# Two edits to a two-block network kernel: when VectorE builds a pair's selection, and where the gates' product runs

## The reference

```python
scores = sigmoid(xt @ router_w)                     # the 8 chosen experts of each token come from these
hb = silu(xb @ w_gate[e]) * (xb @ w_up[e])          # xb: the rows routed to expert e
y = (hb @ w_down[e]) * ws[:, None]
```

```python
x = x + 0.5 * swiglu(rms_norm_2(x, norm_ffn1[l]), ffn1_in[l], ffn1_out[l])
h = rms_norm_2(x, norm_mix[l])
p_rwkv, p_attn, p_gate = split(h @ w_in[l])         # p_gate: 256 x 2048
o_a = rwkv7_mixer(p_rwkv, ...)                      # a linear recurrence over tokens, forward and backward
o_b = diff_attention(p_attn, ...)                   # 4 heads, two softmax maps each
y = einsum('bsgc,gcd->bsgd', stack([o_a, o_b]), w_branch[l])
merged = sum(sigmoid(p_gate) * y, over the two branches)
x = x + merged @ w_out[l]
x = x + 0.5 * swiglu(rms_norm_2(x, norm_ffn2[l]), ffn2_in[l], ffn2_out[l])
```

## Time and profile before

| what | us |
|---|---|
| three runs | 4134.38, 4137.35, 4137.35 |
| their median | 4137.35 |
| the profiled execution's own time | 4137.76 |
| its span in the trace | 4136.1 |
| first block (both layers) | 0 to about 2046 |
| second block (both layers) | about 2046 to the end |
| PE busy | 3485.1 |

### The profile page before, as it was taken

The page is one execution under the profiler, slowest core; times in us unless marked ns, Lnnn a source line. Parts: engine busy times, 40 slices in busy tenths (PEclk is TensorE's granted clock), DMA queues, the critical chain, the costliest instruction groups (busy, mean ns, idle before and its releaser), DMA issues.

```text
span 4136.1 us, 46292 instructions
## 1 busy us (share of the span) xinstructions
PE 3485.1 (84%) x18496; PEld 2414.5 (58%) x18496; DVE 1569.9 (38%) x2703; ACT 842.4 (20%) x1240; POOL 599.4 (14%) x556
## 2 busy tenths in 40 slices
PE   6888999994788899999299958798988994879899
PEld 3754333331566333333098648686978963877688
DVE  4433222224634222222354265531545426554154
ACT  1211111110130111111132221111324223111132
POOL 4402233331440233233100000000000000000000
PEclk8889999997878999999699968779998996877999
DMA  7647999985754899889554300004536430000352
GB/s 264 236 158 279 364 347 354 356 338 197 283 181 168 343 351 353 341 350 358 181 195 153 130 8 1 1 21 147 199 102 225 159 117 21 1 1 13 130 204 102
DMA packets 305420, 799.38 MB, mean 193 GB/s; under 512 B 57030, under 2 KB 155868, under 8 KB 251308
## 3 DMA queue, kind: packets, MB, share of 16 engines
q1 hardware_dynamic: 245804, 727.16, 46.8%
q0 software_dynamic: 58848, 67.05, 4.9%
q10 hardware_dynamic: 544, 2.10, 0.1%
HBM read 989.01 MB, written 53.48 MB: 252 GB/s over the span
## 4 chain that ended last, share of the span: by engine, by line
PE 41%; DVE 6%; ACT 1%; issue 1%; DMA 1%; SPq 0%; DVEq 0%
PE s_bank L1899 12%; PE s_bank L1937 6%; PE s_bank L1887 5%; PE s_bank L2083 2%; PE s_bank L1964 2%; PE s_bank L2098 2%; PE s_bank L2093 1%; PE s_bank L2200 1%; PE s_bank L2210 1%; PE s_bank L2168 1%; PE s_bank L2160 1%; PE s_bank L2071 1%; DMA s_ringA<-in_ffn_in 1%; PE s_bank L2153 1%; PE s_bank L2145 1%
## 5 line engine op out<-in xcount | busy, mean ns | idle before, releaser
L711 PE MATMUL f_bank<-f_ringA,f_arena 128*64 128x512 f32 x3072 | 688.7, 601 | 16.3 <-DMA f_ringA<-in_w_up,f_chosen 10.1
L711 PEld LDWEIGHTS f_bank<-f_ringA,f_arena 128*64 128x64 f32 x3072 | 222.3, 138 | 401.4 <-issue 400.1
L1899 PE MATMUL s_bank<-s_hT_high_parts,s_highA_parts 128*128 128x256 f32 x1408 | 402.7, 286 | 17.7 <-DVE s_hT_parts L2428 17.7
L1899 PE MATMUL s_bank<-s_hT_parts,s_highA_parts 128*128 128x256 f32 x1408 | 402.2, 286 | 0.0
L1899 PE MATMUL s_bank<-s_hT_high_parts,s_ringA_parts 128*128 128x256 f32 x1408 | 402.0, 285 | 0.0
L732 PE MATMUL f_bank<-f_ringB,f_arena 128*64 128x512 f32 x1536 | 346.5, 592 | 1.0 <-DVE f_arena L1473 1.0
L1012 ACT ACTIVATE f_arena<-f_bank 128x512 f32<-128x512 f32 (+1 forms) x362 | 202.1, 587 | 575.1 <-PE f_bank L692 174.2
L1465 DVE TENSOR_TENSOR f_arena<-f_arena,f_bank 128x256 f32<-128x256 f32 x96 | 58.6, 610 | 636.3 <-ACT f_arena L1090 636.3
L1899 PEld LDWEIGHTS s_bank<-s_hT_high_parts,s_highA_parts 128*128 128x128 f32 x1408 | 274.2, 195 | 20.4 <-issue 19.0
L1899 PEld LDWEIGHTS s_bank<-s_hT_parts,s_highA_parts 128*128 128x128 f32 x1408 | 274.3, 195 | 1.4
L1899 PEld LDWEIGHTS s_bank<-s_hT_high_parts,s_ringA_parts 128*128 128x128 f32 x1408 | 274.1, 195 | 0.0
(11 more groups left out here) (393 smaller groups left out, 5361.2 us busy)
## 6 DMA issues: line engine op xcount, KB each, us to landing
f_ringA<-in_w_gate SPq DMA_DIRECT2D x128, 1024.0 KB, 8.7
f_ringA<-in_w_up SPq DMA_DIRECT2D x128, 1024.0 KB, 11.1
f_ringB<-in_w_down SPq DMA_DIRECT2D x128, 1024.0 KB, 12.3
s_ringA<-in_ffn_in SPq DMA_DIRECT2D x88, 1024.0 KB, 7.7
f_ringA<-in_w_ada SPq DMA_DIRECT2D x48, 1024.0 KB, 8.4
s_arena<-in_ffn_out SPq DMA_DIRECT2D x44, 1024.0 KB, 6.0
s_ringA<-in_w_in SPq DMA_DIRECT2D x40, 1024.0 KB, 6.1
f_ringA<-in_w_in SPq DMA_DIRECT2D x28, 1024.0 KB, 10.2
```

What stands on the lines that cost most here:

```text
L711: last = mm(ps[j * CAP:(j + 1) * CAP, :].rearrange("p (h c) -> p h c", h=2), picked[:, b % 2, k, j * CAP:(j + 1) * CAP], gu[j][:, :, k, :] ...
L1899: last = mm(ps[:, t * S:(t + 1) * S], parts_of(wx[:, k, cs_]), parts_of(hx[:, k, :]), start=(k == 0 and x == 0), stop=(k == DT - 1 and x = ...
```

## The change

In the first block `select(b + AHEAD)` moves on VectorE from behind the copies of iteration b to the head of the iteration, ahead of the wait for the SiLU. `take_rows` stays.

In the second block:

- The gates' product is cut into 16 pieces (`half_gates`), each 8 matmul calls. Pieces 0 to 7 stand behind the scores of attention's steps 0 to 7; pieces 8 to 15 behind the chunk steps of the scans, four a direction. The loop over 8 groups after the scans is gone.
- ACT takes groups 0 to 3 as plain copies during attention, one sigmoid over them (2048 columns) behind the set-up of direction 0, and groups 4 to 7 through a sigmoid in the scans. No take waits for `oa_ready` any more.
- `gates` moves into slot 0 of `ringA`. The gate and branch weights use slots 1 and 2 in turn (`slot_of`); `w_out` gets two places of its own in SBUF that the scans have used, so its loads wait for the last Y bank.
- Three instead of one of ffn2's first weights are loaded before `x_ready`.

```diff
@@ first block, VectorE
                 for b in range(PAIRS + 1):
+                    if b + AHEAD < PAIRS:
+                        select(b + AHEAD)
                     if b < PAIRS:
                         dve.wait_ge(silu_ready, b + 1)
...
                     if b + AHEAD < PAIRS:
-                        select(b + AHEAD)
                         take_rows(b + AHEAD)
@@ second block, buffers, banks and slots
-        gates = view(base + 1024, 4096, "p (t s) -> p t s", s=S)
+        gates = ringA[:, 0, :].rearrange("p (t s) -> p t s", s=S)
+        w_out = [view(base + 8192 + 4096 * n, 4096) for n in range(2)]
...
+        for g in range(4):
+            banks.take(("gates", g), 2 + g % 2)
...
+            for g in range(4 + 2 * d, 6 + 2 * d):
+                banks.take(("gates", g), 4 + g % 2)
...
-        for g in range(8):
-            banks.take(("gates", g), g % 4)
...
+        slot_of = [n % slots_A for n in range(a_gate)] + [1, 2] * 3 + [(1, 2, 0)[s % 3] for s in range(STEPS)]
@@ SP
                 def slot_free(n):
-                    if n >= slots_A:
-                        banks.read(sp, last_use[n - slots_A])
+                    before = [i for i in range(n) if slot_of[i] == slot_of[n]]
+                    if before:
+                        banks.read(sp, last_use[before[-1]])
+                    if n == a_ffn2 + 2:
+                        sp.wait_ge(merged, DT)
...
+                banks.read(sp, ("Y", 1, 1))
                 for c in range(2):
-                    load(a_out + c, rows8(slotA(a_out + c)),
-                         a["w_out_2"][l, :, c * 512:(c + 1) * 512].rearrange("(k p) c -> p k c", p=P))
-                load_up(2, 0)
+                    dst = rows8(w_out[c])
+                    src = a["w_out_2"][l, :, c * 512:(c + 1) * 512].rearrange("(k p) c -> p k c", p=P)
+                    for h in range(2):
+                        sp.dma_start(dst[:, h * 4:(h + 1) * 4], src[:, h * 4:(h + 1) * 4]
+                                     ).then_inc(each[f"w_out{c}"], 16)
+                for s in range(3):
+                    load_up(2, s)
                 sp.wait_ge(x_ready, 2)
                 for s in range(STEPS):
-                    if s:
+                    if s >= 3:
                         load_up(2, s)
                     load_down(2, s)
@@ PE
+            def half_gates(i):
+
+                g, t = i // 2, i % 2
+                c = a_gate + g // 2
+                if i % 4 == 0:
+                    landed(c)
+                ps = banks.claim(pe, ("gates", g)) if t == 0 else banks.t[banks.uses[("gates", g)][0]]
+                w, o = rows8(slotA(c)), (2 * (g % 2) + t) * P
+                for k in range(DT):
+                    last = mm(ps[:, t * S:(t + 1) * S], w[:, k, o:o + P], hT[:, k, :],
+                              start=(k == 0), stop=(k == DT - 1))
+                if t:
+                    banks.fill(last, ("gates", g))
...
                         banks.fill(last, ("score", s))
+                        half_gates(s)
                     if s % 2 and s > 1:
...
+                        half_gates(8 + 4 * d + n)
                     pe.wait_ge(sa_ready, 4 * d + 4)
...
-                for g in range(8):
-                    c = a_gate + g // 2
-                    if g % 2 == 0:
-                        landed(c)
-                    o = (g % 2) * 2 * P
-                    ps = banks.claim(pe, ("gates", g))
-                    banks.fill(hidden(ps, rows8(slotA(c))[:, :, o:o + 2 * P]), ("gates", g))
                 pe.wait_ge(oa_ready, 1)
@@ ACT
                         last.then_inc(exp_done, 1)
+                        if s % 2:
+                            take_gates(s // 2, ACT.Copy)
...
+                    if d == 0:
+                        for g in range(4):
+                            banks.evacuated(act, ("gates", g))
+                        f(gates[:, 0:8, :], gates[:, 0:8, :], ACT.Sigmoid).then_inc(gates_ready, 1)
+                    for g in range(4 + 2 * d, 6 + 2 * d):
+                        take_gates(g, ACT.Sigmoid)
 
                 roots(16)
-                for g in range(8):
-                    if g == 0:
-                        act.wait_ge(oa_ready, 1)
-                    take(("gates", g), gates[:, 2 * g:2 * g + 2, :], pair_of, ACT.Sigmoid)
@@ VectorE
-                for g in range(8):
+                dve.wait_ge(gates_ready, 1)
+                for g in range(4, 8):
                     banks.evacuated(dve, ("gates", g))
```

More of the change, by code:

```diff
@@ L1621, in second_block @@
                  "highA_ready", "lowA_ready", "highB_ready", "lowB_ready", "hT_split", "hid_split",
-                 "oa_ready", "merged", "dve_steps", "rows_landed", "arrived"]
+                 "oa_ready", "gates_ready", "w_out0", "w_out1", "merged", "dve_steps", "rows_landed", "arrived"]
         names += [f"bank_filled{i}" for i in range(8)] + [f"bank_freed{i}" for i in range(8)]
@@ L1641, in second_block @@
         merged, dve_steps, arrived = each["merged"], each["dve_steps"], each["arrived"]
+        gates_ready = each["gates_ready"]
         rows_landed = each["rows_landed"]
@@ L1737, in second_block @@
         a_wa = a_gate + 4
-        a_wb, a_out, a_ffn2 = a_wa + 1, a_wa + 2, a_wa + 4
+        a_wb, a_ffn2 = a_wa + 1, a_wa + 2
         last_use = {s: ("u", 0, s) for s in range(STEPS)}
@@ L1743, in second_block, with a_filled @@
         last_use |= {a_wa: ("branch", DT - 1), a_wb: ("branch", DT - 1)}
-        last_use |= {a_out + n: ("out", n, 1) for n in range(2)}
         last_use |= {a_ffn2 + s: ("u", 2, s) for s in range(STEPS)}
         ffn_first = {0: 0, 2: a_ffn2}
+        slot_of = [n % slots_A for n in range(a_gate)] + [1, 2] * 3 + [(1, 2, 0)[s % 3] for s in range(STEPS)]
         def slotA(n):
-            return ringA[:, n % slots_A, :]
+            return ringA[:, slot_of[n], :]
+        def a_filled(eng, n):
+            eng.wait_ge(a_landed[slot_of[n]], 32 * slot_of[:n + 1].count(slot_of[n]))
         def rows8(ap):
@@ L1778, in load @@
                         sp.dma_start(dst[:, h * half:(h + 1) * half], src[:, h * half:(h + 1) * half]
-                                     ).then_inc(a_landed[n % slots_A], 16)
+                                     ).then_inc(a_landed[slot_of[n]], 16)
                 def load_up(f, s):
@@ L1869, in landed @@
             def landed(n):
-                pe.wait_ge(a_landed[n % slots_A], 32 * (n // slots_A + 1))
+                a_filled(pe, n)
             def to_features(key, src, n_banks):
@@ L2204, in _ @@
                 for n in range(2):
-                    landed(a_out + n)
-                    w = rows8(slotA(a_out + n))
+                    pe.wait_ge(each[f"w_out{n}"], 32)
+                    w = rows8(w_out[n])
                     for m in range(MT):
@@ L2229, in take, with take_gates @@
                 banks.free(f(dst, view_(banks.read(act, key)), func, **kw), key)
+            def take_gates(g, func):
+                take(("gates", g), gates[:, 2 * g:2 * g + 2, :], pair_of, func)
             def split_up(k, s):
                 n = ffn_first[k] + s
-                act.wait_ge(a_landed[n % slots_A], 32 * (n // slots_A + 1))
+                a_filled(act, n)
                 if s >= 2:
```

## The result

The changed kernel takes **3979.06 us** (3978.22 to 3982.74, 4 runs) against 4136.94 us (4134.38 to 4137.35, 4 runs) before: ratio 0.962, 95% interval 0.9607 to 0.9633, 158 us less. The forecast was 4037 us, range 3995 to 4090. The direction was right; the gain was half as large again as forecast, and it lies outside the range.

What follows compares the result with a forecast made beforehand. TensorE, busy 84%, was limited differently by stage: selection waits in the first loop, VectorE in attention, the gates' product after the scans. From 4137.76 us, -68 - 81.8 + 19 + 30 = -100.8 gave 4037 us, range 3995 to 4090.

Steps and rivals of the forecast that it cites:

- First part: First block's loop: moving the selection removes the lookup's 0.90 us wait, 77.7 us traced, less 10 for late weights: -68.
- The bound of -78: First block's loop: the most the moved selection could save, all of the lookup's traced wait.
- the 64 of the second part: Second block: us saved with the gates' product change at its best, used for the range's lower end.
- Rival 2: First block's loop: transfers bound it, so the moved selection saves 34 for 68 us; 4071 us, chance 12%.
- What goes after the scans: Y's last bank to branches: 17.3 us for 60.8 without the gates' product, -43.5; cold branches +2.6 a layer.
- Attention: Eight pieces a layer: first head pair's combination after 20.2 us, +9.4; later heads 11.3 us, as now; +9.5 a layer.
- Scans: Four pieces a direction: step 0 +5.9, steps 1 and 2 +1.5 each, step 3 +2.5, Y sums -4; +7.4 a direction.
- if the clock holds: Scan steps 1 and 2: 8.8 us, no change, at a held clock; 12.9, +4, if it falls; +1.5 each taken.
- a rise within each piece: Scans: full-width work raises the clock to 1.00 once per piece, as at 2407.6 in attention; what follows takes about half.
- Rival 1: Clock sags in the scans: each direction +19, attention +15 us a layer; 4094 us, chance 20%.
- Rival 3: Scans and attention: every piece runs whole at 1.2 GHz, making the kernel slower; 4181 us, chance 5%.
- Rival 4: No effect: another wait replaces the selection's, scans and attention eat the 41 us a layer; about 4138 us, chance 2%.

Runs made afterwards that it cites:

- e1_select: The kernel before, with only the selection moved and the second block untouched: 4046.63 us, ratio 0.9782.
- b1_gaps: The changed kernel with attention's eight pieces moved into TensorE's waits and ACT's copies moved accordingly: 3940.76 us, ratio 0.9524.
- e3_block: The changed kernel with each direction's four scan pieces in one block ahead of its first step: 4006.59 us, ratio 0.9685.
- e4_pairs: The changed kernel with two scan pieces at step 0, two at step 2, none at 1 and 3: 4012.41 us.
- e6_bare: b1_gaps with no piece in the scans; those pieces stand in waits outside them: 3993.43 us, ratio 0.965.
- b4_first: b1_gaps with the piece of step 0 ahead of the state products in the first direction only: 3948.01 us, ratio 0.9547.
- b2_ahead: b1_gaps with the piece of step 0 ahead of the state products in both directions: 3945.49 us, ratio 0.9533.
- e2_second: The changed kernel with the selection put back behind VectorE's copies, leaving only the second block's change: 4069.83 us, ratio 0.9836.
- e8_twice_after: The changed kernel with every selection computed twice by VectorE: 3987.55 us.
- b2 to b4: b2_ahead, b4_first, and between them b2_ahead with the second direction's last piece moved behind the Y sums: 3946.64 us, ratio 0.953.

## Why the prediction was right in sign and off in size

1. **First part, forecast -68, measured -88.** The mechanism, the hidden place, the DMA backlog (10 forecast, 8.8 measured) and the weights' rate (377 forecast, 387 measured) were right. The step that failed is "88 x 0.90 = 79; I use the traced 77.7". The gap ahead of L682 in the multiply queue is shorter than what the lookup costs standing alone: from L692 to L711 it is 2.23 us before and 1.08 after, and the load queue's gap (96.2 us) is close to that. e1_select repeats the gain with this edit alone. The bound of -78 was no bound, nor was the 64 of the second part: that part gave 71.4, and beyond 64 lie only terms that are not in its sum (point 6). So the range's lower end, 78 + 64, was too high by both.
2. **Rival 2** (transfers bound the loop) is out: 11.81 us at a share of 0.99, PE without a gap. The prediction cited the Trainium skill's limit of some 358 GB/s against this part, and 387 GB/s over 35 us does not agree with it as a limit of this run. The Trainium skill's "HBM Reference" (section Specifications (TRN2)) has the reason: the figure is each core's share when both cores of a pair stream, and one core alone measures well above it. This kernel's core ran alone, and its rows agree; a run beside a busy core was not made.
3. **What goes after the scans, forecast -43.5 and +2.6 a layer, measured -43.4 and +2.8.** Right, to the cold start of the branches.
4. **Attention, forecast +9.5, measured +9.7 and +10.2.** The first pair was right (20.2 against 20.7 us to the first combination). That the total is right too is partly luck: two later heads cost 0.75 us each more than before, where 11.3 was put "as now", and the last 1.8 us, in no term, go the other way. The reading that VectorE sets the pace of 11.4 us is corrected by b1_gaps: it was in part PE's own low clock.
5. **Scans, forecast +7.4 a direction, measured +1.0.** The failed step is "if the clock holds ... no change; if it falls between pieces, 12.9, +4; I take +1.5 each", with "Step 3: +2.5" and, for the Y sums, "get some full clock: -4". Step 0 cost 5.4 (forecast 5.9), steps 1 to 3 together 1.4 (forecast 5.5), the sums gave 5.8 (forecast 4). The clock held from the first piece to the end of the sums, in all four directions. e3_block, e4_pairs and e6_bare show that the recurring pieces are what holds it. The prediction's own figure for a held clock, 8.8 us a step, was met (8.74); it was given too little weight. This is 6.4 x 4 = 26 us. The ground for a rise within each piece was thin: before 2407.6 PE ran 2.07 us of 128x128 products (L2010) and 2.09 us of 64-row scores (L1995), not the full-width work of a piece. That the clock did rise within the first piece of a direction is right, but not by that row.
6. **Not in the sum at all:** the second direction's preparation begins with the clock in which the sums end, 1.00 instead of 0.50, and takes 4.2 us less a layer. In e3_block, where the sums end at 0.50 again, its first 50 us pass at 0.50, 0.55 and 0.83 (over 6, 24 and 20 us), as in the kernel before (0.50, 0.54, 0.83). But full clock at its start is not enough: in b4_first it starts so too and takes 124.9 us, more than the 123.4 before. What decides how soon the clock comes back there stays open. Another 5.5 us lie over the second block; their cause was not looked for.
7. **Rival 1** (the clock sags in the scans) had the right danger and the wrong distance: it came true only where the pieces were bunched or moved apart (e3_block, e4_pairs, b2_ahead). The Trainium skill's rule behind it ("TensorE: Matmul & The Clock Gate", section A second HAM failure mode), that short idling between groups of matmuls makes the clock swing, told there of a bf16 kernel that cycles through PSUM banks, is not borne out by the changed kernel's scans, which idle 0.9 us in each step at a steady 1.00. **Rival 3** is out: in the scans the pieces of steps 1 to 3 take 3.67 to 3.72 us, and only the first of a direction 5.6 to 5.7. **Rival 4** is out by e1_select and e2_second.

## What to carry to other kernels

Read a wait of TensorE in both of its queues: at the one place tried here, the weight load stood idle longer than the multiply (1.11 us for 0.90), and the longer gap was nearer to the price (1.14 us). Where narrow products run at half clock beside a chain on another engine, wide work that has to be done anyway can be nearly free with a piece in every step, and dear if it is bunched or taken out. Whether narrow filler would do the same was not tried. Price a stretch together with what comes behind it, since that starts at the clock the stretch leaves and may get it back sooner or later (b4_first). And put a piece into a wait ahead of the consumer, not between producers that another engine is waiting for: that and ACT's copies moved along made 3979 into 3941 us.

## What was not expected of the hardware

- PE busy for 92% of 26 us did not hold 2.4 GHz (e3_block), nor did 93% over a whole direction. The busy share in a profile does not tell which clock a stretch will get.
- The clock can rise early or late in the same instruction stream. In b1_gaps the preparation of the first direction took 123.0 us in the first layer and 128.9 in the second. Windows of 12 us that start 24.0 us into that preparation in both; by their counts, less work is done in the second:

```profile
2354.30:2366.30 12.00, 11.44 (x64) 10.19 (x64) 6.90 (x17) 2.39 (x4) 0.00 (x0) 0.86 0.00 0
3341.60:3353.60 12.00, 12.00 (x43) 10.15 (x44) 3.63 (x10) 2.39 (x4) 0.00 (x0) 0.50 0.00 0
```

  The same stretch took 128.4 us in the first layer of e4_pairs and of e8_twice_after, and 123.3 in the changed kernel's. It is worth some 5 us a time. The runs of b2 to b4 scatter over 9 to 15 us where b1_gaps stays within 3; that the late rise makes this scatter is likely, but not shown. What decides between early and late stays open.
- The weights passed at 387 GB/s over 35 us with PE busy for all of it; the 351 of the kernel before was set by PE, not by the transfers.
